# Three seven-product units instead of two in the gate and up projections of a macaron transformer block

## The reference, cut to what matters

```
h = h + 0.5 * (silu(n @ w_gate) * (n @ w_up)) @ w_down      n = rms_norm(h)
n: 256 x 2048    w_gate, w_up: 2048 x 5632    w_down: 5632 x 2048
```

## Time and profile before

| | |
|---|---|
| time, median of 3 runs | 1835.25 us (1835.12 to 1835.49) |
| span of the profiled execution, first to last instruction | 1834.2 us |
| PE busy | 1819.6 us, 99% of the span |
| DVE busy | 1505.4 us, 82% |
| ACT busy | 995.2 us, 54% |
| mean granted TensorE clock | 0.999 |
| moved by DMA | 380.36 MB, 207 GB/s |

### The profile page before, as it was taken

How to read it: one execution, slowest core, us unless ns; L and a number is a source line. 1 busy time by engine, 2 the same in 40 slices (tenths; PEclk the granted TensorE clock), 3 DMA queues, 4 the chain that set the end, 5 groups by cost and what they waited for, 6 DMA issues and landing times. The chain is left out here.

```text
span 1834.2 us, 29749 instructions
## 1 busy us (share of the span) xinstructions
PE 1819.6 (99%) x10696; PEld 1546.4 (84%) x10696; DVE 1505.4 (82%) x1755; ACT 995.2 (54%) x1181; POOL 11.1 (1%) x23
## 2 busy tenths in 40 slices
PE   9999999999999999999999999999999999999998
PEld 7888888888888888999998878888888888888886
DVE  5888888888988985788867866688888888889996
ACT  7555555545555655754535655545555555555554
POOL 1000000000000000000000000000000000000000
PEclk9999999999999999999999999999999999999999
DMA  7677666777766778564443557677777677676664
GB/s 252 221 219 228 219 216 215 220 229 236 233 202 204 225 224 267 173 184 140 138 116 106 176 171 261 180 232 231 229 224 232 216 227 222 217 240 195 209 208 157
DMA packets 207851, 380.36 MB, mean 207 GB/s; under 512 B 16016, under 2 KB 35728, under 8 KB 207504
## 3 DMA queue, kind: packets, MB, share of 16 engines
q1 hardware_dynamic: 206768, 377.08, 65.7%
q10 hardware_dynamic: 480, 1.97, 0.3%
q0 software_dynamic: 512, 0.06, 0.0%
HBM read 360.19 MB, written 18.87 MB: 207 GB/s over the span
## 5 line engine op out<-in xcount | busy, mean ns | idle before, releaser
L402 ACT CAST whi<-raw 128x1024 fp32r<-128x1024 f32 (+1 forms) x648 | 675.1, 1047 | 700.8 <-DVE raw L1476 189.6
L411 DVE TENSOR_TENSOR wlo<-raw,whi 128x1024 fp32r<-128x1024 f32 (+1 forms) x648 | 771.7, 1212 | 208.4 <-ACT whi L402 194.5
L428 PE MATMUL psA<-whi,xh 128*128 128x512 f32 (+1 forms) x572 | 219.5, 384 | 0.5 <-DVE wlo L411 0.5
L428 PE MATMUL psA<-whi,xl 128*128 128x512 f32 (+1 forms) x572 | 219.2, 383 | 0.0
L428 PE MATMUL psA<-wlo,xh 128*128 128x512 f32 (+1 forms) x572 | 219.1, 383 | 0.0
L428 PE MATMUL psB<-whi,xh 128*128 128x512 f32 x544 | 211.7, 389 | 0.0
L428 PE MATMUL psB<-wlo,xh 128*128 128x512 f32 x544 | 211.6, 389 | 0.0
L428 PE MATMUL psB<-whi,xl 128*128 128x512 f32 x544 | 211.6, 389 | 0.0
L428 PEld LDWEIGHTS psA<-whi,xh 128*128 128x128 f32 x572 | 107.4, 188 | 21.6 <-DVE wlo L411 0.7
L428 PEld LDWEIGHTS psA<-whi,xl 128*128 128x128 f32 x572 | 107.4, 188 | 21.2
L428 PEld LDWEIGHTS psA<-wlo,xh 128*128 128x128 f32 x572 | 107.4, 188 | 21.0
(11 more groups left out here) (520 smaller groups left out, 3447.3 us busy)
## 6 DMA issues: line engine op xcount, KB each, us to landing
raw<-in_ffn_w_gate SPq DMA_DIRECT2D x176, 512.0 KB, 4.5
raw<-in_ffn_w_up SPq DMA_DIRECT2D x176, 512.0 KB, 4.6
raw<-in_ffn_w_down SPq DMA_DIRECT2D x176, 512.0 KB, 4.6
raw<-in_w_in SPq DMA_DIRECT2D x80, 512.0 KB, 3.6
raw<-in_w_out SPq DMA_DIRECT2D x32, 512.0 KB, 4.2
quads_dram<-stage SPq DMA_DIRECT2D x88, 128.0 KB, 4.2
stage<-quads_dram SPq DMA_DIRECT2D x22, 512.0 KB, 4.3
x<-in_x SPq DMA_DIRECT2D x4, 512.0 KB, 7.5
```

Of the source, the lines that this page charges most:

```text
L402: nc.scalar.copy(whi[:, slot, :, 0:ncol], raw[:, slot, :, 0:ncol]).then_inc(hi_ready, 1)
L411: nc.vector.tensor_tensor(wlo[:, slot, :, 0:ncol], raw[:, slot, :, 0:ncol], whi[:, slot, :, 0:ncol].bitcast(F32), ALU.subtract).then_inc(l ...
L428: mm = nc.tensor.matmul(ps[:, tb, 0:ncol], lhs[:, k0 + t, tok], rhs[:, slot, t, 0:ncol], start=(first and t == 0 and p == 0 and tb != open ...
```

## The change

`GATE_UNITS` goes from 2 to 3: in each of the ten chunks after the first, two plain groups (gate 4 and up 4 of the former order) become part of a third unit, and the order of the sixteen groups is: four plain, unit, two plain, unit, two plain, unit, two plain. Before, it was four plain, unit, three plain, unit, five plain. The step that copies Q1 and makes the closing sums is bound to group 15 instead of 14, since a unit now holds groups 12 and 13; the load that brings the transposed tiles back is issued before group 14 instead of 13. In the first chunk the up groups are taken in another order (`FIRST_UP`: rows of the units first), so that the token sums, now in batches of three, may overwrite their tiles after three up groups instead of four. The token sums take more room, so `shares` reaches beyond the table of constants: two small tiles are moved behind it and a spacer of 256 columns is added.

```diff
--- before.py
+++ after.py
@@ -42,10 +42,12 @@
 FC = F // COLS
 DC = D // COLS
 
-GATE_UNITS = 2
+GATE_UNITS = 3
 GATE_PAIR = 2
-CHUNK = ([("gate", j) for j in (0, 1, 4, 5)] + [("unit", 0)] + [("gate", j) for j in (6, 7)] + [("up", 0)] + [("unit", 1)]
-         + [("up", j) for j in (1, 4, 5, 6, 7)])
+CHUNK = ([("gate", j) for j in (0, 1, 5, 6)] + [("unit", 0)] + [("gate", 7), ("up", 0)] + [("unit", 1)]
+         + [("up", 1), ("up", 5)] + [("unit", 2)] + [("up", j) for j in (6, 7)])
+FIRST_UP = list(range(GATE_PAIR, GATE_PAIR + GATE_UNITS))
+FIRST_UP += [j for j in range(GD) if j not in FIRST_UP]
 UNITS = ((7, 7), (7, 8))
 GATE_TOTAL = GATE_UNITS * (FC - 1)
 GATE_STEPS = 5 * (FC - 1)
@@ -78,6 +80,7 @@
 
 
 CONST_WIDTH = 2816
+BEYOND = 256
 
 
 def down_order(f, m):
@@ -189,6 +192,9 @@
         cos_i, sin_i = consts[:, 768:1024], consts[:, 1024:1280]
         cos_q, sin_q = consts[:, 1280:1536], consts[:, 1536:1792]
         to_channels = consts[:, 1792:2816].rearrange("p (t c) -> p t c", c=P)
+        token_scale = sb("token_scale", [P, S])
+        same_r = sb("same_r", [P, P], F32R)
+        sb("beyond_consts", [P, BEYOND])
         prow = sb("prow", [P, P])
         pcol = sb("pcol", [P, P])
         prow2 = sb("prow2", [2, P])
@@ -289,8 +295,6 @@
         shares = at("shares", [P, TB, COLS], consts, plus=4 * P + 24 * P * GATE_UNITS)
         xl_sum = at("xl_sum", [P, KD, S], xl)
         hl_sum = at("hl_sum", [P, KF, S], arena, plus=KF * S * 4)
-        token_scale = sb("token_scale", [P, S])
-        same_r = sb("same_r", [P, P], F32R)
         widx_scale = sb("widx_scale", [P, TB])
         att_scale = sb("att_scale", [P, TB])
         widx = sb("widx", [P, TB, IDX_HEADS])
@@ -662,7 +666,7 @@
                     for kind, j, g in chunk_items():
                         if g == 11:
                             quads_store(sp, f, n - 1)
-                        if g == 13:
+                        if g == PER - 2:
                             quads_load(sp, f, n - 1)
                         for i, w in enumerate((w_gate, w_up) if kind == "unit" else (w_gate,) if kind == "gate" else (w_up,)):
                             pair = GATE_PAIR + j if kind == "unit" else j
@@ -674,8 +678,8 @@
                         xq_store(sp, 2, 2)
                     if f == 1 and j == 4:
                         xq_load(sp, 2, 2)
-                for j in range(GD):
-                    load_group(sp, rows(w_up, j * KT)[:, :, 0:COLS], base, 0, PER, GD + j)
+                for i, j in enumerate(FIRST_UP):
+                    load_group(sp, rows(w_up, j * KT)[:, :, 0:COLS], base, 0, PER, GD + i)
             chunk(0)
             with sp.Fori(1, FC) as n:
                 chunk(n)
@@ -739,7 +743,7 @@
                         nc.scalar.wait_ge(col_step, n * (4 * GATE_UNITS) + (4 * unit + 2))
                         split_hi(base, n, PER, g + 1)
                         unit_hi(n, unit)
-                    if g == PER - 2:
+                    if g == PER - 1:
 
                         nc.scalar.wait_ge(quads_stored, n * 64 + 64 * f * FC)
                         nc.scalar.wait_ge(unit_used, n * GATE_UNITS + FIRST_UNIT[f])
@@ -814,7 +818,7 @@
         def batch(b, f):
 
             if f is None:
-                return 2, slice(0, 2)
+                return GATE_UNITS, slice(0, GATE_UNITS)
             n = min(2, max(UNITS[f]) - 2 * b)
             return n, slice(2 * b, 2 * b + n)
 
@@ -944,7 +948,7 @@
                         split_lo(base, 0, PER, j)
                     first_dve(j)
                     if j == PER - 3:
-                        nc.vector.wait_ge(group_used, base + GD + GATE_PAIR + GATE_UNITS)
+                        nc.vector.wait_ge(group_used, base + GD + GATE_UNITS)
                         halves_dve(xh, xl, xl_sum, x_sum, GATE_PAIR // 2, sum_number(f))
                     if j == PER - 1:
                         halves_lo(xh, xl, xl_sum, x_sum_lo, x_sum_hi, x_sum, GATE_PAIR // 2, sum_number(f))
@@ -1084,8 +1088,8 @@
                                    between=(lambda: turn_x(0, 2)) if f == 0 and j == 0 else None)
                 if f == 0:
                     turn_params()
-                for j in range(GD):
-                    project_tokens(psB, xh, xl, base, 0, PER, GD + j, j * KT, j == 0, j == GD - 1)
+                for i, j in enumerate(FIRST_UP):
+                    project_tokens(psB, xh, xl, base, 0, PER, GD + i, j * KT, i == 0, i == GD - 1)
 
             def chunk(n):
```

## The result

The changed kernel takes 1904.64 us in the median (1902.49 to 1905.49, four runs) beside 1835.37 for the kernel before (1835.12 to 1836.13): a ratio of 1.0374, 95% interval 1.0359 to 1.0389. It is slower by 69.3 us, and its profiled span is 1903.7 us against 1834.2 (the profiled run took 1905.49). The forecast was 1889, the range 1873 to 1911.

A forecast was written before the change was run, and what follows sets the result against it. The prediction took the matmuls on TensorE (PE) to set the pace. It summed -13.6 removed, +58.6 boundary waits, +8.1 inside passes and +0.5 for other edits to +53.6 us: 1889 us, range 1873 to 1911.

The forecast's parts named there:

- What is removed, 13.6 us: In 20 chunks, two plain groups of 24 matmuls become a unit of 21: 13.6 us less for PE, pass 41.48.
- The boundary chain: From T, a chunk's last unit done, ACT and DVE relay to next group 0: 2.93 us wait, 20 times, 58.6 us.
- Inside a pass: DVE begins each pass without a lead, so PE waits around unit 0: 0.45 us in 18 passes, 8.1 us.
- the near tie: Before unit 0, low part 4 ends at T + 19.03 and PE wants it at 19.09: just in time.
- The clock: At boundaries, pauses of 2.7 us without a matmul may lower PE's clock; the forecast stayed just clear of that, 1889.
- rival 1: The clock falls at a third or so of the boundaries: 7 x (2.72 - 0.45) = +16, 1905 us; chance 0.14.
- The page's rule: Advice against matmul gaps of about 3 us; a boundary pause of 2.7 us was taken to stay just clear.
- Edits at next to nothing: Down projections 0.25 us per layer, 0.5 in all; first chunk's batches and order, later load and moved tiles nothing.
- Rivals 2 and 3: DVE not regaining its lead inside passes, +27, 1916, chance 0.10; the boundary chain staying hidden, 1821.65, chance 0.04.
- rival 2: Inside 18 passes, unit 2's loads or DVE come 1.5 us later than laid out: +27, 1916 us; chance 0.10.

The follow-up runs named there:

- o_tiles_first: i_in_the_gap with both steps of the turned tiles moved before the copy and closing sums, and the transposes behind low part 7: 1824.10 us, ratio 0.9935 to the kernel before.
- a_converts_later: The changed kernel with ScalarE converting the turned tiles behind the high part of the next chunk's first group instead of in front of it: 1888.98 us.
- b_one_ahead: The changed kernel with both parts of the next chunk's group 0 made before the copy of Q1 and the closing sums: 1873.35 us.
- k_in_the_gap_pool: i_in_the_gap with the low parts of the turned tiles made on GpSimd instead of VectorE: 1864.94 us.
- i_in_the_gap: The changed kernel with the next groups 0 and 1 split after the Q1 copy, around the closing sums, and a later turned-tile load: 1841.93 us.
- h_two_units_two_behind: The kernel before, still with two units, its second unit moved to where the third now stands, closing sums at group 15: 1915.59 us.
- c_two_ahead: The changed kernel with high parts of next groups 0 and 1 before the Q1 copy, low parts before and behind the closing sums: 1856.72 us.
- e_four_behind: The changed kernel with one plain group between units and four behind the last, closing sums at group 14, turned tiles stored before group 12: 1891.80 us.
- d_close_at_14: The changed kernel with the copy of Q1 and the closing sums put back to group 14: 1938.21 us.
- n_converts_later_pool: a_converts_later with the low parts of the turned tiles made on GpSimd instead of VectorE: 1897.34 us.

## Why the prediction was right, point by point

- **What is removed, 13.6 us.** Right: a pass without waits is 41.48 us (o_tiles_first).
- **The boundary chain.** Right in every link. PE starts at T + 8.03 against 8.11; silu starts at T + 3.39 against 3.47, the first high part at 5.57 against 5.66, the low part at 6.75 against 6.83. The hand-over from ACT to the first closing sum took 0.03 us instead of 0.12, which is the whole difference.
- **Inside a pass.** Right in size and place: 0.5 us against 0.45 in a pass without a fall, nearly 0.2 within unit 0 and 0.3 before group 6. Boundary and inside together: 65.8 measured in the chunks, plus 13.6 for the removed matmuls, less 12 x 1.1 for the clock, is 66 us; the forecast had 58.6 + 8.1 = 66.7.
- **What the near tie meant.** Missed. The prediction noted that low part 4 came just in time and drew nothing from it; for the change itself nothing hung on it. a_converts_later and b_one_ahead show that the boundary wait and the list up to unit 0 are one chain: a link removed at the boundary alone gives 0.2 us a pass, not 1.03.
- **The clock.** This is the step that put the time above the forecast: it took the granted clock to stay at 1.00 over a pause of 2.7 us and priced the clock at nothing, and 13 to 14 of the 16 us are the clock's; the rest is in the down projections and the mixing layer. It stood as rival 1, with a chance of 0.14 and 1905 us, and it is what happened. That 1905 is so near 1904.64 is luck: there were 12 falls at 1.1 to 1.2 us where the rival had 7 at 2.3, and 3 us more than forecast lie outside the chunks. Its price took a whole group at half the clock, 2.72 us more, less the 0.45 inside the pass. The subtraction was right: in the pass from 1573.66 the late starts in unit 0 and before group 6 are gone, 0.5 us. The first number was too large: the first four groups of that pass take 1.6 us more than in the pass from 1439.08, since only some eight matmuls run at the low clock, not twelve. The row at the end of the trace, a fall 2.4 us after the last matmul, was a warning that the pause was long enough. It was no threshold: after the last matmul the granted clock leaves 1.00 2.2 us later in k_in_the_gap_pool and 5.0 us later in i_in_the_gap.
- **The page's rule.** The Trainium skill, "TensorE: Matmul & The Clock Gate", section "Why this matters for your kernels", advises against idle gaps of about 3 us between bursts, and the prediction read that as leaving a pause of 2.7 us just clear. The measurement decides: behind pauses of 2.57 us the clock fell at 12 of 20.
- **Edits at next to nothing.** The first chunk was right, 0.1 and 0.0 us. The down projections grew by 1.1 and 1.2 us, not by 0.25 each: PE starts late at three units in layer one and at two in layer two (0.67 us of wait at 1755.60, the longest). The prediction's reason, that DVE begins them without a lead, fits but was not tested. The mixing layer grew by 1.2 us, which the prediction didn't have. Two of PE's waits for DVE there are longer, 1.42 us in place of 0.80 at its start and 1.26 in place of 0.45 soon after; why was not tried.
- **Rivals 2 and 3.** Neither: in 17 of 18 passes unit 2 started 10.20 us after unit 1, the time of the matmuls. In the other it was 10.41, and there DVE had stood 2.08 us for unit 2's up load: the case of rival 2, once and for 0.2 us. And h_two_units_two_behind shows that the order alone makes the boundary wait.

## What to carry to other kernels

A list of matmuls may be dense and still rest on a relay between the other engines that is hidden only by what stands behind the last unit; before shortening or reordering, add up that relay and compare it with the work that covers it. When it is uncovered, don't just cut a link: find the next point at which the slower engine is due, since a gain before a tie is lost after it, and move steps into the idle time that the relay itself leaves (ACT while DVE closes, DVE while ACT copies). Price a pause of the matmul engine with the clock in mind: here one of 2.6 us could bring the low clock back, and one of 1.6 us did not. And an expectation met in its number is not yet met in its cause: twice here a kernel's time was what a rival gave (c_two_ahead, e_four_behind), and the waits in the trace named something else.

## What the runs showed of the hardware that was not expected

- The same pause doesn't always lower the clock. Pauses of 2.56 to 2.59 us did so at 12, 11 and 13 of 20 boundaries in three kernels, pauses of 3.0 us at 20 of 20, and pauses of 1.6 us or less at no boundary. A wait of 2.03 us inside the mixing layer of a_converts_later was followed by a fall too, as was one of 2.85 us at the same place in d_close_at_14 (for a_converts_later the granted clock is 0.98 in the first half microsecond after PE went on at 738.83, and 0.59 in the next). What decides between two equal pauses was not tried. A fall cost 1.1 to 1.2 us on PE's path. Whether their number varies from run to run was not looked at; if it does, that would make up part of the spread of the changed kernel's runs (1902.5 to 1905.5).
- The clock's fall can come after the pause. At six of the twelve boundaries of the changed kernel PE had been running for 0.9 to 1.5 us again when the granted clock left 1.00, as at 1574.87 behind the pause that ended at 1573.66.
- One GpSimd `tensor_tensor` of 128 x 512 float32 took 2.08 us in k_in_the_gap_pool and 1.78 in n_converts_later_pool, beside VectorE's two-input operations, and in k these lost more (2.2 us) than the work taken from VectorE (1.2).
